# Sliding-window attention in units of four heads that begin inside the query projections, and output projections in two halves of K

## What is computed

```python
def second_block(x, c, ...):
    for i in range(4):
        kind, j = i % 3, i // 3                     # 0: swa, 1: gla, 2: fox
        sh1, sc1, g1, sh2, sc2, g2 = split(silu(c) @ ada_w[i] + ada_b[i], 6)
        h = modulate(rmsnorm(x, norm_gain[i, 0]), sh1, sc1)
        y = (swa_mixer, gla_mixer, fox_mixer)[kind](h, ...)      # each ends in  o @ w_o
        x = x + g1 * y
        h = modulate(rmsnorm(x, norm_gain[i, 1]), sh2, sc2)
        x = x + g2 * ((silu(h @ w_g) * (h @ w_u)) @ w_down)      # FFN
    return rmsnorm(x, final_norm)

def swa_mixer(h, w_in, sinks, w_o):                 # layers 0 and 3
    q, k, v = split(h @ w_in, [1024, 1280])         # 16 query heads of 64, 4 key/value heads
    q, k = rope(q), rope(k)
    # queries attend in blocks of 128 rows to their own and the block before (window 128)
    scores = where(mask, q @ k.T * 64 ** -0.5, -inf)
    probs = softmax(concat([scores, sink]))[..., :-1]
    return (probs @ v).reshape(B, S, 1024) @ w_o
```

## Time and profile before

| | before |
|---|---|
| median of 3 runs | 2427.35 us |
| the profiled execution's own time | 2432.57 us |
| its span | 2430.8 us |
| PE busy | 2240.5 us (92%) |
| DVE busy | 1631.8 us (67%) |
| ACT busy | 1040.4 us (43%) |
| POOL busy | 199.0 us (8%) |
| chain that ended last | PE 35%, DVE 6%, ACT 2%, issue 2% |

### The profile page before, as it was taken

One profiled execution on the slowest core, in us unless ns is written; L12 is line 12 of the kernel. 1 busy time (PEld: TensorE's weight loads), 2 busy tenths in 40 slices (PEclk: granted clock), 3 DMA queues, 4 the chain that ended last, 5 costly groups with the idle time before them and its releaser, 6 DMA issues. The chain is left out here.

```text
span 2430.8 us, 33994 instructions
## 1 busy us (share of the span) xinstructions
PE 2240.5 (92%) x13701; PEld 1972.0 (81%) x13701; DVE 1631.8 (67%) x2343; ACT 1040.4 (43%) x1705; POOL 199.0 (8%) x212
## 2 busy tenths in 40 slices
PE   6999998799999989878999986999999999979997
PEld 5999887689998877766998864899886799857996
DVE  5576677666667677677898665778745654667554
ACT  4444444344544444445333341434433444445432
POOL 1000001000000001110000122001100001110000
PEclk8999999899999999989999998999998999989999
DMA  8866675567677655443999520588631555524561
GB/s 280 286 207 221 219 238 169 184 199 235 214 229 221 219 176 180 164 152 110 314 358 341 200 96 35 173 311 291 224 118 44 165 186 187 185 79 147 174 212 66
DMA packets 305537, 474.68 MB, mean 195 GB/s; under 512 B 20416, under 2 KB 168314, under 8 KB 305380
## 3 DMA queue, kind: packets, MB, share of 16 engines
q1 hardware_dynamic: 295252, 440.68, 54.6%
q0 software_dynamic: 10128, 31.83, 4.4%
HBM read 466.00 MB, written 6.42 MB: 194 GB/s over the span
## 5 line engine op out<-in xcount | busy, mean ns | idle before, releaser
L147 DVE TENSOR_TENSOR wlo<-raw,whi 128x1024 fp32r<-128x1024 f32 x640 | 775.0, 1243 | 237.3 <-ACT whi L141 235.2
L141 ACT ACTIVATE whi<-raw 128x1024 fp32r<-128x1024 f32 x640 | 643.1, 1052 | 150.3 <-DMA raw<-in_ffn_w_gu 77.4
L135 PE MATMUL G<-HTh,whi 128*128 128x256 f32 x2304 | 662.7, 288 | 3.1 <-DVE pool L155 2.1
L135 PE MATMUL G<-HTl,whi 128*128 128x256 f32 x2304 | 653.2, 283 | 0.0
L135 PE MATMUL G<-HTh,wlo 128*128 128x256 f32 x2304 | 653.1, 283 | 0.0
L135 PEld LDWEIGHTS G<-HTh,whi 128*128 128x128 f32 x2304 | 443.2, 192 | 9.4 <-issue 6.2
L135 PEld LDWEIGHTS G<-HTl,whi 128*128 128x128 f32 x2304 | 443.4, 192 | 2.3
L135 PEld LDWEIGHTS G<-HTh,wlo 128*128 128x128 f32 x2304 | 443.0, 192 | 0.0
L141 ACT ACTIVATE pool<-G 128x512 f32<-128x512 f32 (+1 forms) x224 | 122.4, 569 | 618.8 <-PE G L135 562.4
L135 PE MATMUL G<-whi,HTh 128*128 128x512 f32 (+1 forms) x768 | 309.3, 403 | 15.0 <-ACT HTh L141 10.4
L135 PE MATMUL G<-whi,HTl 128*128 128x512 f32 (+1 forms) x768 | 299.5, 390 | 2.1 <-DVE HTl L155 1.5
(11 more groups left out here) (149 smaller groups left out, 2500.7 us busy)
## 6 DMA issues: line engine op xcount, KB each, us to landing
raw<-in_ada_w SPq DMA_DIRECT2D x192, 512.0 KB, 5.7
raw<-in_ffn_w_gu SPq DMA_DIRECT2D x352, 256.0 KB, 5.0
raw<-in_w_in SPq DMA_DIRECT2D x224, 256.0 KB, 4.2
raw<-in_w_in SPq DMA_DIRECT2D x96, 512.0 KB, 4.9
raw<-in_ffn_w_down SPq DMA_DIRECT2D x88, 512.0 KB, 5.5
pool<-mod_rows POOLq DMA_DIRECT2D x24, 512.0 KB, 5.2
raw<-in_swa_w_in SPq DMA_DIRECT2D x24, 512.0 KB, 5.2
raw<-in_gla_w_in SPq DMA_DIRECT2D x24, 512.0 KB, 4.9
```

Of the source, the lines that this page charges most:

```text
L135: return self.e.matmul(out, a, b, start=start, stop=stop, skip_group_check=True) if self.e else self
L141: return self.e.activation(out, a, func, bias=bias, scale=scale, accum_out=accum) if self.e else self
L147: return self.e.tensor_tensor(out, a, b, op) if self.e else self
```

## The change

The weights of each output projection come in another order: first K rows 0 to 511 for both column units, then the rest; the pieces are the same in number and size. The new `out_proj` replaces the `gemm` and `Apart` of all four layers. It holds all four G banks, one for each (column unit, row tile), does the first half of K for all of them with a `tick` after each six matmuls, then calls `end`, and then does the second half inside `turn`.

In the two SWA layers the 16 units of two heads become 8 units `win` of four heads, (kv, t). Logits of all live units go through A0 (stages 0 and 1) and everything after through A1 (stages 3 to 6); a unit whose bank is held by another stays where it is. There are three places. The query units are `Apart` now, so row tile 0 of a unit is finished after four parts. Keys and queries are transposed for each row tile apart, three ticks after their rope was issued (`soon`, `tick`), and units are appended as soon as the queries of their row tile are issued. `swa_layer` returns when the units of the first query unit (kv 0 and 1, blocks 0 to 3 of `OT`) are done; the others go on beside the first half of the output projection and are finished in `end`.

```diff
-    for u in range(2):
-        add(("wo2", l, u), wo, D, [(u * 512, 512)])
+    for kh in range(2):
+        for u in range(2):
+            add(("wo2", l, u, kh), wo[kh * 512:kh * 512 + 512, :], 512, [(u * 512, 512)])
...
-            {"diff": self.diff, "mem": self.mem, "dil": self.dil, "swa": self.swa, "fox": self.fox,
-             "gla": self.gla}[u.kind](u)
+            if {"diff": self.diff, "mem": self.mem, "dil": self.dil, "win": self.win, "fox": self.fox,
+                    "gla": self.gla}[u.kind](u) is False:
+                continue
             u.s += 1
             if u.s == u.n:
                 self.live[u["j"]] = None
+    def tick(self):
+        for x in self.soon:
+            x[0] -= 1
+        due = [x for x in self.soon if x[0] <= 0]
+        self.soon = [x for x in self.soon if x[0] > 0]
+        for x in due:
+            x[1]()
+        self.step()
...
-    def swa(self, u):
-        self.pair(u, self.h_swa)
+    def win(self, u):
+        i, sl = u.s, u["sl"]
+        if i in (0, 3):
+            if self.owner[i // 3] is not None:
+                return False
+            self.owner[i // 3] = u
+        if i == 1:
+            u["nm"], u["su"] = self.smc(4), self.smc(4)
+        elif i == 2:
+            u["rc"] = self.smc(4)
+        self.h_win(u)
+        if i == 1:
+            self.owner[0], self.slots[0].ps_free = None, [u.ev("ve", "s")]
+        elif i == 6:
+            self.owner[1], self.slots[1].ps_free = None, [u.ev("ve", "lo")]
+            self.OT.write(2 * u["kv"], 2, [u.ev("ve", "lo")], (u["t"],))
+            sl.S_free, sl.W_free = [u.ev("pe", "tr")], [u.ev("pe", "pv")]
+            u["st"]["t"].append(u.ev("ve", "lo"))
+            u["st"]["n"][u["kv"] // 2] += 1
...
+        kT = self.mk_blk(4)
+        def kv_T(t, ready):
+            g = self.gbank()
+            tr, done = self.new("pe_tr"), self.new("ac_tr")
+            self.h_kvT(g, t, kvb, ready, kT, self.gfree[g], tr, done)
+            self.gfree[g] = [done]
+            kT.tok = kT.tok + [done]
+        def ev_kv(t, ps, full):
+            read, done = rope_bank(ps, t, kvb, t * 512, 4, full)
             copied = self.new("ac_ev")
-            self.h_copy(kvb.a[:, g * 512 + 256:g * 512 + 512], ps[:, 256:512], full, kvb.w + [read], copied)
+            self.h_copy(kvb.a[:, t * 512 + 256:t * 512 + 512], ps[:, 256:512], full, kvb.w + [read], copied)
             kvb.tok = kvb.tok + [done, copied]
+            self.soon.append([3, lambda: kv_T(t, done)])
             return [copied]
-        self.swah = cb, msk, snk, tms, tsk, kvb, rope_bank
+        self.swah = cb, msk, snk, tms, tsk, kvb, kT, rope_bank
         return self.apart(self.HT, ("swa", l, 2), ev_kv)
     def swa_layer(self, l):
-        M = self.M
...
-        def kv_T():
-            for n2 in range(2):
+        cb, msk, snk, tms, tsk, kvb, kT, rope_bank = self.swah
+        st = {"t": [], "n": [0, 0]}
+        seat = Seat(self)
+        self.place[:] = self.slots + [seat]
+        self.live[:] = [None] * 3
+        qTs = []
+        for u in range(2):
+            qt, qT = self.mk_blk(4), self.mk_blk(4)
+            qTs.append(qT)
+            def q_T(t, ready, u=u, qt=qt, qT=qT):
                 g = self.gbank()
                 tr, done = self.new("pe_tr"), self.new("ac_tr")
-                self.h_kvT(g, n2, kvb, kT, self.gfree[g], tr, done)
+                self.h_qT(g, t, qt, ready, qT, self.gfree[g], tr, done)
                 self.gfree[g] = [done]
-                kT.tok = kT.tok + [done]
...
-        for u in range(2):
...
-            def ev_q(g, ps, full, qt=qt):
...
+                qT.tok = qT.tok + [done]
+                if t:
+                    qt.release([tr])
+                for kv in (2 * u, 2 * u + 1):
+                    self.pend.append(Unit("win", 7, ("swa", l, kv, t), kv=kv, t=t, q=qT, tq=done, k=kT, v=kvb, st=st,
+                                          mask=msk, snk=snk, tms=tms, tsk=tsk))
+            def ev_q(t, ps, full, qt=qt, q_T=q_T):
+                read, done = rope_bank(ps, t, qt, t * 512, 8, full)
+                self.soon.append([3, lambda: q_T(t, done)])
                 return [read]
-            self.gemm(self.HT, 0, ("swa", l, u), D, "TT", ev_q)
...
-            def q_T(u=u, qt=qt):
...
-                for n2 in range(2):
...
-                for kv in (2 * u, 2 * u + 1):
-                    for t in range(2):
-                        for hp in range(2):
-                            self.pend.append(Unit("swa", 7, ("swa", l, kv, t, hp), kv=kv, hp=hp, t=t, q=qT, k=kT, v=kvb,
...
-        self.widen(4)
-        self.drain(lambda: not self.busy())
...
-        for b in qTs + [kT, kvb, cb]:
...
+            q = self.apart(self.HT, ("swa", l, u), ev_q)
+            for t in range(2):
+                for i in range(4):
+                    q(t, i)
+        while self.soon or st["n"][0] < 4:
+            self.tick()
+        def end():
+            self.drain(lambda: not self.busy())
+            self.place[:], self.live[:] = self.slots, [None] * 2
+            for j, sl in enumerate(self.slots):
+                sl.ps_free = self.slots[j].ps_free
+            seat.close()
+            for b in qTs + [kT, kvb, cb]:
+                b.release(st["t"])
+        return end
...
+    def out_proj(self, l, end):
+        gs = {(u, t): self.gbank() for t in range(2) for u in range(2)}
+        for g in gs.values():
+            self.gheld[g] = True
+        for u in range(2):
+            for h in range(2):
+                n, lo = self.take(("wo2", l, u, 0))
+                for t in range(2):
+                    done, g = (("pe_first", "pe_w")[t], n), gs[(u, t)]
+                    self.h_mm1(self.OT, 2 * h, n % NSPL, lo, t, g, h == 0, False, self.gfree[g], done)
+                    self.tick()
+                self.give(n, done)
+                for b in (2 * h, 2 * h + 1):
+                    self.OT.free[b] = [done]
+        if end:
+            end()
+        gb = self.mod_row(l, 16)
+        N = self.modulated(l, 1)
+        ws = {}
+        def part(t, u, h, late=False):
+            def f():
+                if t == 0:
+                    ws[(u, h)] = self.take(("wo2", l, u, 1))
+                n, lo = ws[(u, h)]
+                done, g = (("pe_first", "pe_w")[t], n), gs[(u, t)]
+                self.h_mm1(self.OT, 4 + 2 * h, n % NSPL, lo, t, g, False, h == 1, [], done)
+                if t:
+                    self.give(n, done)
+                    for b in (4 + 2 * h, 5 + 2 * h):
+                        self.OT.free[b] = [done]
+                def resid():
+                    self.gfree[g] = self.residual(gb, u, t, self.M.GB[g][:, :], done, N, t == 1 and not late)
+                    self.gheld[g] = False
+                    if t and u:
+                        gb.release(N.nx[0] + N.nx[1])
+                if h and late:
+                    self.later.append(resid)
+                elif h:
+                    resid()
+            return f
+        last = ([part(0, u, h) for u in range(2) for h in range(2)], [part(1, 0, 0)],
+                [part(1, 0, 1), part(1, 1, 0), part(1, 1, 1, True)])
+        self.turn(last, self.normed(N), self.ffn_head(l))
...
         for l in range(4):
-            (self.swa_layer, self.gla_layer, self.fox_layer)[l % 3](l)
...
-            def ev(u):
...
-            self.gemm(self.OT, 0, ("wo2", l, 0), D, "TT", ev(0))
...
+            end = (self.swa_layer, self.gla_layer, self.fox_layer)[l % 3](l)
+            self.out_proj(l, end)
...
+    def h_win(self, u):
+        e, sl, i, kv, t = self.e, u["sl"], u.s, u["kv"], u["t"]
+        K, lg, pt = (t + 1) * P, self.M.AB[0], self.M.AB[1]
         if i == 0:
             q = u["q"].a.rearrange("p (n c) -> p n c", n=4)
             kt = u["k"].a.rearrange("p (n c) -> p n c", n=4)
-            for x in u["q"].tok + u["k"].tok + sl.ps_free:
+            for x in [u["tq"]] + u["k"].tok[:t + 1] + self.slots[0].ps_free:
                 e.wait_ge(*self.at(x))
             for n in range(2):
-                mm = e.matmul(sl.ps[:, n * 256:n * 256 + K], q[r0:r0 + 64, (2 * kv + n) % 4, t * P:t * P + P],
...
+                for hp in range(2):
+                    r0 = 64 * hp
+                    mm = e.matmul(lg[:, hp, n * K:n * K + K], q[r0:r0 + 64, (2 * kv + n) % 4, t * P:t * P + P],
+                                  kt[r0:r0 + 64, kv, 0:K], True, True)
             mm.then_inc(*self.up(u.ev("pe", "qk")))
         elif i == 3:
-            self.pair_tr(u)
...
-            for x in u["v"].tok:
+            S = sl.S[:, 0:4 * K + 4].rearrange("p (n k) -> p n k", n=4)
+            for x in [u.ev("ve", "w")] + self.slots[1].ps_free:
                 e.wait_ge(*self.at(x))
             for kc in range(t + 1):
-                v = u["v"].a[:, kc * 512 + 256 + kv * 64:kc * 512 + 256 + kv * 64 + 64]
...
+                for n in range(4):
```

(50 more changed lines are left out.)

136 lines of the change are left out of this document (56 added, 80 removed).

## The result

The change makes the kernel slower: 2461.31 us (median of 4 runs, 2457.64 to 2461.92) against 2427.81 (4 runs), ratio 1.0132, 95% interval 1.0114 to 1.0149, which is +33.5 us. The forecast was +13.8.

A forecast was written before the change was run, and what follows sets the result against it. The prediction took the SWA attention to be a chain from PE over DVE and ACT back to PE, with no engine full. Its terms, 8.2 + 3.4 + 2.2 = +13.8 us, gave 2441 us, range 2416 to 2457.

The forecast's parts named there:

- (f): Output projection, between the halves of K: the last two t = 1 units pass one after the other through A1, 10.5 us.
- the 2.5 us taken off in layer 3: Layer 3, (c) to (f): taken as 2.5 us shorter than in layer 0, being without the sums of modulation.
- term 1: Second query unit of the SWA layers: query projections end 17.5 us later in layer 0, 14 in layer 3.
- term 3: Turns of the four layers: +0.8 us each, +1.5 more in layer 0, 2.5 off in GLA, sum +2.2.
- (b): Second query unit: the second unit's transposes wait for the first unit's OTl to free A1, 7.5 us, 4 in layer 3.
- (a): Second query unit: the third unit's logits wait for the copy of row tile 1's queries on ACT, 4 us.
- The clock: Rival, chance 0.15: interleaved matmuls of (a) to (e) run at 1.2 GHz after PE stands still, giving 2451 us.
- (c): After the query projections: the fourth unit's W copy stands behind the fifth's exponentials, 7.5 us.
- (d): Before the first half of K: the other t = 1 unit waits for A1, then passes through alone, 6.5 us.
- (e): First half of K: 16.5 us of matmuls and other units' work, plus 7.5 us of waits for W copies.
- (g): Second half of K in the output projection: 11 us and 1 for a cold start, 12 us.
- hiding: Rival, chance 0.2: PE never waits inside the second query unit, so interleaving hides the attention, giving 2414 us.

The follow-up runs named there:

- e4: As the change, but each step advances the oldest four-head unit first instead of the youngest: 2444.7 us.
- e7: Kernel before, with query units and transposes by row tile and its two-head units (own banks) begun inside the first query unit: 2433.3 us.
- e3: As the change, but no attention unit begins before the last query matmul: 2483.6 us.
- e6: As the change, but two places instead of three, a pair of banks for each unit, and oldest unit first: 2452.9 us.
- e11: As the change, but two places, a pair of banks for each unit, and every unit finished before the output projection of before: 2424.7 us.
- e13: As the change, but a unit in its last stage is advanced ahead of the others, the rest youngest first: 2445.2 us.
- e9: As the change, with A0 and A1 still shared, but two places instead of three: 2451.2 us.

## Why the prediction was wrong

The direction was right, and so were the waits at the first hand-over of A1; the size was not: +13.8 against +33.5, outside of the range (2416 to 2457). What failed is the low clock behind the waits, put at nothing in term 1; the second waits for A1 in (f); the 2.5 us taken off in layer 3; and the turn of layer 0 in term 3. By its own steps:

- **(b), the wait for A1**: 7.5 and 4 us said, 7.30 and 4.23 measured, with the releaser named. Right, the 4 partly by luck: the lines written under it make 8.7 - 3 = 5.7 us without sums or `wlo`. **(a)**: 4 said, 2.40 and 2.45 measured; the first transposes waited another 1.91, which had no term. But the query stretch of before had idle time of its own (3.0 and 2.0 us), which the prediction did not take off: idle time grows by 9.4 and 7.4 us, where 11.5 and 8 were said.
- **The clock in term 1** is the first term that failed. PE is busy 10.6 us longer in the query stretch (45.36 against 34.79) and 10.9 in layer 3, where 6 were said. The work moved in was about right: the rows of logits, transposes of weights and queries, and products sum to 9.6 us in layer 0, against 2.9 before, so 6.7. The rest is the projection matmuls behind the waits: six of them take 2.7 to 2.9 us in place of 1.65 at three places, 3.6 us, and this had no term. The clock was a rival, where it belonged in the sum: with it the stretches grow by 20.0 and 18.3 us, not 17.5 and 14.
- **(c) and (d)**: 14 said, 14.4 measured (1090.0 to 1104.43, the first output matmul; four units are through A1 by then and two more are begun). **(e)**: 24 said, 24.5 measured. **(g)**: 12 said, 11.8 measured. Right, with the wait for W of 5.37 us where 5 were said.
- **(f), the last two units through A1**: 10.5 said, 14.6 measured (1128.9 to 1143.5), and 14.7 in layer 3. The wait of 3.66 us (3.70 in layer 3) for the `OTl` of the sixth unit through A1, behind the softmax of the seventh, had no term: the mechanism of (b), not looked for a second time.
- **"In layer 3 I take 2.5 less"** was wrong: 64.5 us against 65.3, so the sums of modulation on DVE mattered little. With (f) that makes 6.5 us in layer 3.
- **Term 3**: +2.2 said. From the last output matmul (for GLA and FOX the first) to the first `G<-HTh,whi` matmul of the FFN the turns take 4.3, 0.3, 0.9 and 0.8 us more. Layer 0 carries the eight `ones` matmuls and 2.12 us idle, since `ada_sums` may not run while all G banks are held; the prediction had a bank wait there instead. In GLA the 1.81 us idle did go, but other waits took its place, so the 2.5 us off were not there.
- Of the rivals, hiding did not happen: it was to be decided by an A1 wait of under 1 us, and that was 7.30. The clock fell as its rival said, but that rival alone gives 2451.

The measured terms sum to 15.5 + 14.2 + 6.4 = 36.1 us, the two profiles differ by 29.3. Between the FFN of layer 0 and the output projection of GLA, which the change leaves alone, the profile after is 6.5 us quicker (19.65 us late at the one, 13.1 at the other). Part of it is a better clock: 0.97 against 0.94 in the GLA projections (53.93 against 57.49 us). e4 shows 6.6 us there and e7 4.6, e3 0.4. Its cause stays open. The other 4.2 us, from 29.3 to the 33.5 of the medians, are there because the profiled execution of before took 4.8 us more than the median of 2427.81, that of the change 0.6.

The experiments price the design itself: third place and shared banks cost 33.0 us. The prediction took both as given, and priced the queue in front of A1 at its first hand-over only.

## What to carry to other kernels

A bank, or any buffer, that units take in turn ties the end of one unit to the start of the next. If the instruction that frees it, or one that this needs (`OTh` on ACT here), stands in an engine's queue behind a younger unit's softmax, PE pays for that softmax: here 7.30, 4.23, 3.66 and 3.70 us. Give each unit in flight its own bank before adding units. Where that can't be, advance the unit that is about to free the bank before the ones that wait for it. Check the same queue at every later hand-over, not only at the first, and try the order again after each such change (e6). Fewer and larger instructions (13 us less of DVE) came with at most 3.7 us of gain (e11).

Before a difference of a few us is put down to an edit, compare the stretches that it touches and those that it does not.

## What the runs showed that was not expected

- The order in which units are advanced moved the time by 16.6 us one way with shared banks and by 24.6 us the other way with own banks.
- To fill an idle PE brought the clock from 0.50 to 1.00 behind the wait and doubled the matmuls in 3.5 us, and the two layers got only 2.6 us shorter.
- The attention of FOX took 39.9 us in two traces (granted clock 0.89 in e13) and 44 us in the others (0.77 in the change), in a stretch that no edit touches.
- A wait that PE has for W on ACT (23.5 us in e9) vanished when nothing on ACT was made faster, only when two units went in step.
